# The first weight block after a norm, multiplied tile by tile

## The reference

```python
def rms_norm(x, g):
    y = xf * lax.rsqrt(jnp.mean(jnp.square(xf), axis=-1, keepdims=True) + EPS)
    return (y * g.astype(jnp.float32)).astype(x.dtype)

def modulate(h, shift, scale):
    return h * (1.0 + scale) + shift

def swiglu(h, w1, w3, w2):
    return (jax.nn.silu(h @ w1) * (h @ w3)) @ w2

    for i in range(DEPTH):                     # 2
        h = modulate(rms_norm(x, norm1_g[i]), sh1, sc1)
        ...                                    # mixer: latent attention, or
        else:
            mix = odd_mixer(h @ b_w_in[j], ...) @ b_w_out[j]
        x = x + g1 * mix
        x = x + g2 * swiglu(modulate(rms_norm(x, norm2_g[i]), sh2, sc2), ffn_w1[i], ffn_w3[i], ffn_w2[i])
```

## Time and profile before

| | us |
|---|---|
| time, median of 3 runs | 2678.46 |
| lowest and highest of these | 2672.28, 2682.69 |
| the profiled execution's own time | 2674.23 |
| its span in the trace | 2672.4 |
| mean granted TensorE clock of that execution | 0.947 |
| TensorE busy | 2296.8 (86%) |
| VectorE busy | 654.5 (24%) |
| ScalarE busy | 356.1 (13%) |

### The profile page before, as it was taken

How to read it: one execution, slowest core, us unless ns; L and a number is a source line. 1 busy time by engine, 2 the same in 40 slices (tenths; PEclk the granted TensorE clock), 3 DMA queues, 4 the chain that set the end, 5 groups by cost and what they waited for, 6 DMA issues and landing times. The chain is left out here.

```text
span 2672.4 us, 35780 instructions
## 1 busy us (share of the span) xinstructions
PE 2296.8 (86%) x14459; PEld 1216.6 (46%) x14460; DVE 654.5 (24%) x1445; ACT 356.1 (13%) x597; POOL 126.6 (5%) x182
## 2 busy tenths in 40 slices
PE   6999878798888882997678878888498999888999
PEld 3333364443334331333443222322355777665776
DVE  2000276531000006123653200000443000292001
ACT  0000131211111111002421111111043000010000
POOL 1000001000000002100100000000210000000000
PEclk9999989899999995998889999999799999898999
DMA  8888722599999984875159999998441444433442
GB/s 284 320 299 306 266 80 66 207 413 423 423 423 422 423 353 167 313 258 225 50 217 421 422 423 422 423 423 374 147 158 63 155 146 156 154 123 119 149 157 79
DMA packets 176769, 698.29 MB, mean 261 GB/s; under 512 B 14085, under 2 KB 72326, under 8 KB 114097
## 3 DMA queue, kind: packets, MB, share of 16 engines
q1 hardware_dynamic: 162512, 648.98, 62.5%
q0 software_dynamic: 8512, 25.83, 3.1%
q10 hardware_dynamic: 5664, 22.37, 2.3%
HBM read 673.87 MB, written 22.20 MB: 260 GB/s over the span
## 5 line engine op out<-in xcount | busy, mean ns | idle before, releaser
L1480 PE MATMUL bank<-ring,arena 128*32 128x512 f32 (+1 forms) x3072 | 358.3, 614 | 74.5 <-DMA ring<-moe_w_up 47.6
L444 PE MATMUL bank<-ring,actT 128*128 128x512 f32 x768 | 343.9, 601 | 3.7 <-DMA ring<-c_w_qkv 1.4
L2526 PE MATMUL bank<-actT,ring 128*128 128x256 f32 x1408 | 311.8, 383 | 2.0 <-PEq L2632 1.0
L2526 PEld LDWEIGHTS bank<-actT,ring 128*128 128x128 f32 x1408 | 270.6, 192 | 47.9 <-issue 11.3
L1480 PEld LDWEIGHTS bank<-ring,arena 128*32 128x32 f32 x3072 | 100.7, 113 | 327.1 <-issue 325.6
L1497 PE MATMUL bank<-arena 128*32 128x512 f32 (+1 forms) x2048 | 226.6, 594 | 25.7 <-ACT arena L1568 24.7
L444 PEld LDWEIGHTS bank<-ring,actT 128*128 128x128 f32 x768 | 142.6, 191 | 204.6 <-issue 204.6
L1608 DVE TENSOR_TENSOR arena<-arena,bank 128x512 f32<-128x512 f32 x32 | 22.0, 687 | 612.6 <-ACT arena L1566 612.6
L1924 PEld LDWEIGHTS bank<-arena 128*128 128x128 bf16 x2448 | 140.5, 99 | 32.3 <-issue 26.8
L2538 PE MATMUL bank<-ring,arena 128*128 128x512 f32 x352 | 154.3, 592 | 0.0
L1924 PE MATMUL bank<-arena 128*128 128x128 bf16 x2448 | 146.3, 222 | 4.8 <-DVE arena L1600 4.8
(11 more groups left out here) (433 smaller groups left out, 1925.0 us busy)
## 6 DMA issues: line engine op xcount, KB each, us to landing
ring<-moe_w_gate SPq DMA_DIRECT2D x128, 1024.0 KB, 24.1
arena<-moe_w_down SPq DMA_DIRECT2D x128, 1024.0 KB, 21.8
ring<-ada_w SPq DMA_DIRECT2D x96, 1024.0 KB, 7.9
ring<-ffn_w SPq DMA_DIRECT2D x66, 1024.0 KB, 5.3
ring<-moe_w_up SPq DMA_DIRECT2D x64, 1024.0 KB, 24.1
actT<-moe_w_up SPq DMA_DIRECT2D x64, 1024.0 KB, 24.6
made_scratch<-arena ACTq DMA_DIRECT2D x32, 512.0 KB, 7.7
ring<-ab_w_in SPq DMA_DIRECT2D x14, 1024.0 KB, 7.6
```

The lines of the kernel that those rows point to most:

```text
L444: mm = nc.tensor.matmul(self.bank[g % 6][:, :], lhsT(m, k), halves[k // 4][:, k % 4, :], start=(k == 0), stop=(k == KT - 1))
L1480: mm = nc.tensor.matmul(bank[j // 2][Q * q:Q * q + Q, :], A(XS + P * kt + Q * q, Q), weights(j, own, q, k * DE, DE), start=(kt == 0), stop ...
L2526: mm = nc.tensor.matmul(bank[2 * (j % 2) + which][:, f * SEQ:(f + 1) * SEQ], w[:, k, f * P:(f + 1) * P], self.actT[:, k * T:k * T + SEQ], ...
```

## The change

In each of the three seams the 16 matmuls of 256 tokens on the next stage's first weight block become 32 matmuls of 128 tokens. The 16 on tile 0 are issued between tile 0's transposes and tile 1's, still in the old stage; the 16 on tile 1 are the first work of the new stage. The new helper is `tile_products`, called by `first_gateup` (both feed-forwards) and `first_in` (the convolution). It waits for the block's load and, for tile 0, for two counts of `zT_ready`, which ScalarE's copies L2494 now raise. The block's slot is still released after its last matmul, in the new stage. So that tile 0's product has a bank that is free, the feed-forward's gate and up of even steps go to banks 2 and 3, of odd steps to 0 and 1, the other way round from before.

```diff
-                for t in range(2):
-                    self.entry_turn(pe, t, turn_to)
+                self.entry_turn(pe, 0, turn_to)
+                self.first_gateup(pe, 0)
+                self.entry_turn(pe, 1, turn_to)
...
-            self.nc.scalar.activation(self.put_pure(t, h), dims(turn_to(t, h)[:, :], [P, 4], [1, P]), ACT.Copy)
+            self.nc.scalar.activation(self.put_pure(t, h), dims(turn_to(t, h)[:, :], [P, 4], [1, P]), ACT.Copy).then_inc(sm["zT_ready"].up(), 1)
+
+    def tile_products(self, pe, item, t, out):
+
+        self.arrived(pe, item)
+        w = self.slot(item)
+        for f in range(2):
+            for k in range(KT):
+                mm = self.nc.tensor.matmul(out[:, f * SEQ + t * P:f * SEQ + t * P + P], w[:, k, f * P:(f + 1) * P],
+                                           self.actT[:, k * T + t * P:k * T + t * P + P], start=(k == 0), stop=(k == KT - 1))
+        return mm
+
+    def first_gateup(self, pe, t):
+
+        if t == 0:
+            pe.wait_ge(self.sem["zT_ready"].sem, self.sem["zT_ready"].at(2))
+        mm = self.tile_products(pe, self.used, t, self.bank[2])
+        if t:
+            mm.then_inc(self.weights_used.up(), 1)
...
+                    if j == 0:
+                        self.first_gateup(pe, 1)
                     for which in range(2):
+                        if j == 0 and which == 0:
+                            self.frees(self.used, self.weights_used)
+                            self.used += 1
+                            continue
...
-                                mm = nc.tensor.matmul(bank[2 * (j % 2) + which][:, f * SEQ:(f + 1) * SEQ], w[:, k, f * P:(f + 1) * P],
+                                mm = nc.tensor.matmul(bank[2 - 2 * (j % 2) + which][:, f * SEQ:(f + 1) * SEQ], w[:, k, f * P:(f + 1) * P],
...
-                for t in range(2):
-                    self.entry_turn(pe, t, turn_to)
+                self.entry_turn(pe, 0, turn_to)
+                self.first_gateup(pe, 0)
+                self.entry_turn(pe, 1, turn_to)
```

More of the change, by code:

```diff
@@ L2493, in entry_take, with first_in @@
             act.wait_ge(sm["z_turned"].sem, sm["z_turned"].at(2 * t + h + 1))
-            self.nc.scalar.activation(self.put_pure(t, h), dims(turn_to(t, h)[:, :], [P, 4], [1, P]), ACT.Copy)
+            self.nc.scalar.activation(self.put_pure(t, h), dims(turn_to(t, h)[:, :], [P, 4], [1, P]), ACT.Copy).then_inc(sm["zT_ready"].up(), 1)
[13 more added lines that the diff above has]
+            mm.then_inc(self.weights_used.up(), 1)
+    def first_in(self, pe, t):
+        if t == 0:
+            pe.wait_ge(self.sem["zT_ready"].sem, self.sem["zT_ready"].at(2))
+        return self.tile_products(pe, self.used, t, self.bank[0])
     def plan_ffn(self, l):
@@ L2561, in _ @@
                 if then_row is not None:
-                    for t in range(2):
-                        self.entry_turn(pe, t, turn_to)
+                    self.entry_turn(pe, 0, turn_to)
+                    self.first_in(pe, 0)
+                    self.entry_turn(pe, 1, turn_to)
             @block.sync
@@ L2587, in _ @@
                         act.wait_ge(h_ready.sem, h_ready.at(j - 1))
-                    nc.scalar.activation(A(SG + 512 * (j % 2), 512), bank[2 * (j % 2)][:, :], ACT.Silu).then_inc(silu_done.up(), 1)
+                    nc.scalar.activation(A(SG + 512 * (j % 2), 512), bank[2 - 2 * (j % 2)][:, :], ACT.Silu).then_inc(silu_done.up(), 1)
                 if then_row is not None:
@@ L2601, in _ @@
                         dve.wait_ge(down_done.sem, down_done.at(j - 1))
-                    nc.vector.tensor_tensor(A(H + 512 * (j % 2), 512), A(SG + 512 * (j % 2), 512), bank[2 * (j % 2) + 1][:, :],
+                    nc.vector.tensor_tensor(A(H + 512 * (j % 2), 512), A(SG + 512 * (j % 2), 512), bank[3 - 2 * (j % 2)][:, :],
                                             ALU.mult).then_inc(h_ready.up(), 1)
@@ L2647, in _ @@
                     w = self.slot(self.used)
-                    for f in range(2):
+                    if j == 0:
+                        mm = self.first_in(pe, 1)
+                    for f in range(2 if j else 0):
                         for k in range(KT):
```

## The result

The changed kernel takes 2661.45 us in the median of 4 runs (2659.53 to 2663.96), the kernel before 2677.19 us in runs beside it: a ratio of 0.9943 with a 95% interval of 0.9928 to 0.9959, 15.7 us less. Two later series of runs gave 0.9928 (0.9910 to 0.9946) and 0.9939 (0.9925 to 0.9953). The forecast was 2672.3 us with a range of 2663 to 2681.

What follows compares the result with a forecast made beforehand. The prediction took TensorE to bound the second block, with its idle and low-clock time at three seams to be won. Moved work of 5.0 us plus 1.2 us of clock gave 2678.46 - 6.2 = 2672.3 us, range 2663 to 2681.

Steps and rivals of the forecast that it cites:

- What bounds: Second block: TensorE sets the time; its idle and low-clock time at three seams can be won, VectorE's norm unchanged.
- term 1: Each seam: half the first block's work moves into TensorE's idle time, saving 1.67 us per seam, 5.0 us in all.
- What it adds: In the seams: tile 0's products last 2.0 us (high clock) or 3.75 us (low), hidden under VectorE's norm, costing 0.
- The cover of 2.2 us: Before tile 1's transposes: VectorE's norm of tile 1 hides tile 0's products with at least 2.2 us to spare.
- term 2: TensorE's clock at the seams: low stretches sometimes shortened, gaining 1.2 us, a seventh of the possible 8.4 us.
- the clock stays up: Rival: products between the tiles hold the high clock through all seams, gaining 13.4 us, giving 2665.1 us; chance 0.08.
- Loads don't bind: Rival denied here: each narrow matmul takes its weight load's 0.192 us, gaining only 1.1 us, giving 2677.4; chance 0.12.
- The later low stretch: Rival: clock falls later and stays low as long, slowing the new stages; 0.8 us slower, 2679.3 us; chance 0.10.
- No overlap: Rival: tile 0's products are held until tile 1 is ready, losing 0.1 us per seam, 2678.8 us; chance 0.03.
- The weight loads, the exchanged banks and ScalarE's signals: At the seams: the wait for the block's load, swapped banks and new signals were each expected to cost 0.

Runs made afterwards that it cites:

- e2: Changed kernel, but tile 0's products in the gap go unused and the new stage multiplies the whole first block again, wide; 2668.86 us, ratio to before 0.9956.
- e3: Changed kernel with only column half 0 of the block (16 records) multiplied for tile 0 in the gap; 2669.69 us, ratio to before 0.9967.
- e4: Changed kernel plus five unused wide products (10 records) ahead of tile 0's transposes at seams 2 and 3; 2662.64 us.
- e5: Changed kernel plus unused products ahead of tile 0's transposes (seams 2, 3) and half the second weight block for tile 0 in every gap; 2657.83 us, ratio to before 0.9922.
- e7: Changed kernel plus unused products ahead of tile 0's transposes (seams 2, 3) and behind tile 0's products (all seams); 2660.29 us, ratio to before 0.9938.
- e6: Changed kernel plus half the second weight block for tile 0 in every gap, without unused products; 2660.61 us, ratio to before 0.9939.

## Why the prediction was wrong

- **What bounds** and where the time lies: right. TensorE, three seams, VectorE's norm of tile 1 as the cover; VectorE's part did not change. One reading was loose and carries nothing: in the clock row slices 35 and 37 dip, with seams 2 and 3, but the slice of seam 1 (the 31st) is a 9.
- **The step that failed: the count in term 1.** "One block: 16 x 0.216 = 3.45 us before, 16 x 0.1115 = 1.78 us now." The spacing of both kinds was right: 32 narrow take 3.81 us, (3.81 - 0.275) / 31 = 0.114 each. The number was taken from the code and the order of instructions, the durations from rows that count two records for each float32 product. A block is 32 records, term 1 is 3.34 us per seam and 10.0 in all. The record counts show it directly, the difference between e2 and the changed kernel (3.18, 2.67 and 3.37 us) bears the size out, and e3, which moves 16 records, gives about what was predicted for 16.
- **What it adds:** products start 0.1 us behind ScalarE's second copy, as said. They last 3.84 us at the high clock and 6.2 and 6.1 at seams 2 and 3, not 2.0 and 3.75. The cover of 2.2 us "at the tightest" is therefore gone: at seam 2 tile 1's transposes follow the products without a pause, at 2307.29, where VectorE would have had its half ready some 0.45 us earlier (L2480 starts 0.74 us ahead of the transposes at seam 1 before, and the line, now L2481, starts at 2306.09 here). At seam 3 the same reckoning gives 0.4 us. It is a small loss in a large gain.
- **The clock (term 2):** mis-sized as well, at 1.2 us, a seventh of 8.4 that no row gave. It was meant for 2 us of products, for which e3 leaves 1.8. For the work really there the seams gave 17.4 - 10.0 = 7.4 us, near the upper end of 8.4. The expectation "that it mostly still falls, somewhat later, and rises again when it does now" was wrong for the work really there: at seam 1 it did not fall in the changed kernel, and at seams 2 and 3 it rose in the gap. In e3, with half the products, all three new stages begin at the low clock. The same miscount made the rival "the clock stays up" look weak: "the 3.1 to 3.9 us of idle time that are left" were 1.3 at seam 1 and none at the others.
- **The rivals.** "The clock stays up" is nearest to what happened, with its moved work doubled: 10.0 + 7.4. It is not quite that: the clock is up at the head of all three stages, but still falls in the gaps of seams 2 and 3. Whether transposes count for the clock, which was an argument for this rival, no run separates. Loads don't bind (3.81 us, not 6.1, for 32). The later low stretch did not come in the changed kernel, but e4 has it, at about the price of that rival, half of the low time that moves into the new stage. No overlap: not so.
- The weight loads, the exchanged banks and ScalarE's signals cost nothing that any row shows: ahead of tile 0's products TensorE waits for ScalarE's copy L2495, never for a load. A small load does show, at the end of seam 2, where the convolution's first small transposes come earlier now:

```profile
2320.53 0.44 PE L2674 MATMUL bank<-misc,arena 37*128 37x37 f32 x4 [0.28 <-DMA arena<-b_conf_ln_b]
```


The right count was at hand: the row of wide matmuls at seam 1 could have been followed to the first down product (x128 for four blocks).

## What to carry to other kernels

When a row's mean or spacing is multiplied by a count, take the count from the same rows: a float32 product on TensorE is two records here, a transpose one. Work put into TensorE's idle time paid twice here, once by leaving the path and once by where the clock's low stretch then lay; gaps filled to their end (e5, e7) came out shorter than gaps filled at their beginning (e4). Where run to run noise is larger than the effect, lengths between two fixed instructions of the trace can show what medians do not, but the clock can fall differently from one execution to the next (e2, e6), so such a length wants more than one profile.

## What the runs showed of the hardware

- A float32 product 128x128 by 128, 256 or 512 columns shows as two records, spaced by 0.1115, 0.216 and 0.43 us at the high clock: in proportion to the columns, although a weight load's record lasts 0.19 us. So loads of neighbours overlap down to 128 columns.
- Making TensorE faster in a gap can make a seam longer (e4: +1.7 and +2.4 us at two seams), since it then stands idle just before the work that counts. By its time e4 can't be told from the changed kernel (ratios to before of 0.9935 and 0.9943). Dummy work at that place took it back (e7: 2.4 and 2.55 us).
- Products whose result nobody uses made the kernel faster: by 9.8 us in the medians (e2, ratio 0.9956, 0.9940 to 0.9973), of which the seams show 6.5.
- The same work in the gap did not always have the same effect on the clock: through seam 1 it stayed high in four profiles and fell in a fifth (e2).
